# Block products on sums of blocks for six of the eleven chunks of each gated feed-forward (one Trainium2 core)

## What is computed

```
def swiglu(h, wg, wu, wd):
    return (jax.nn.silu(h @ wg) * (h @ wu)) @ wd

for l in range(DEPTH_2):                       # 2 layers
    h = rmsnorm(x, g[0])
    x = x + 0.5 * rmsnorm(swiglu(h, ffn_wg[l, 0], ffn_wu[l, 0], ffn_wd[l, 0]), g[1])
    ...                                        # mixer
    h = rmsnorm(x, g[4])
    x = x + 0.5 * rmsnorm(swiglu(h, ffn_wg[l, 1], ffn_wu[l, 1], ffn_wd[l, 1]), g[5])
```

## Time and profile before

| | |
|---|---|
| runs | 1431.85, 1432.91, 1433.77 us |
| profiled execution | span 1431.2 us, first to last instruction |
| TensorE busy | 1392.6 us, 97% |
| TensorE weight loads busy | 1157.8 us, 81% |
| VectorE busy | 926.0 us, 65% |
| ScalarE busy | 758.1 us, 53% |
| GpSimd busy | 79.3 us, 6% |
| mean granted TensorE clock | 0.993 |

### The profile page before, as it was taken

How to read it: one execution, slowest core, us unless ns; L and a number is a source line. 1 busy time by engine, 2 the same in 40 slices (tenths; PEclk the granted TensorE clock), 3 DMA queues, 4 the chain that set the end, 5 groups by cost and what they waited for, 6 DMA issues and landing times.

```text
span 1431.2 us, 19205 instructions
## 1 busy us (share of the span) xinstructions
PE 1392.6 (97%) x7039; PEld 1157.8 (81%) x7039; DVE 926.0 (65%) x1401; ACT 758.1 (53%) x1249; POOL 79.3 (6%) x133
## 2 busy tenths in 40 slices
PE   4999999999999999999899999999999999999998
PEld 4878877999988888887778888888888877788886
DVE  5677787799777554479986555476545556675453
ACT  4456746755456444366576444465444467574442
POOL 3011100000000000021300000000000100000000
PEclk9999999999999999999999999999999999999999
DMA  9887656477645765544355765547555373565550
GB/s 352 279 293 263 195 173 195 146 268 245 227 146 176 231 196 181 177 133 148 118 173 178 226 199 181 176 134 257 183 185 197 121 210 118 191 230 182 188 165 30
DMA packets 177596, 274.36 MB, mean 192 GB/s; under 512 B 6465, under 2 KB 120897, under 8 KB 177505
## 3 DMA queue, kind: packets, MB, share of 16 engines
q1 hardware_dynamic: 170800, 250.87, 53.2%
q0 software_dynamic: 5552, 20.20, 4.6%
q10 hardware_dynamic: 1153, 2.07, 0.4%
HBM read 272.05 MB, written 1.06 MB: 191 GB/s over the span
## 4 chain that ended last, share of the span: by engine, by line
PE 78%; DVE 4%; issue 1%; ACT 1%; POOL 0%; DVEq 0%; POOLq 0%; ACTq 0%
PE psum L2552 22%; PE psum L2554 22%; PE psum L2553 22%; PE psum L2595 2%; PE psum L2594 2%; PE psum L2592 2%; PE psum L2797 1%; DVE w_lo L2147 1%; PE psum L2649 1%; PE psum L2721 1%; PE psum L2750 0%; DVE attn L2324 0%; PE psum L2664 0%; DVE work L2301 0%; PE psum L2703 0%
## 5 line engine op out<-in xcount | busy, mean ns | idle before, releaser
L2147 DVE TENSOR_TENSOR w_lo<-raw,w_hi 128x1024 fp32r<-128x1024 f32 (+1 forms) x312 | 371.9, 1235 | 115.4 <-ACT w_hi L1936 114.5
L2552 PE MATMUL psum<-w_hi,hT_hi 128*128 128x512 f32 x888 | 357.3, 402 | 6.4 <-DVE hT_lo L2247 3.7
L1936 ACT ACTIVATE w_hi<-raw 128x1024 fp32r<-128x1024 f32 (+1 forms) x312 | 310.8, 1050 | 98.6 <-PE psum L2554 62.2
L2554 PE MATMUL psum<-w_hi,hT_lo 128*128 128x512 f32 x888 | 347.8, 392 | 0.0
L2553 PE MATMUL psum<-w_lo,hT_hi 128*128 128x512 f32 x888 | 347.3, 391 | 0.0
L2552 PEld LDWEIGHTS psum<-w_hi,hT_hi 128*128 128x128 f32 x888 | 167.8, 189 | 45.5 <-issue 10.2
L2554 PEld LDWEIGHTS psum<-w_hi,hT_lo 128*128 128x128 f32 x888 | 167.5, 189 | 36.5
L2553 PEld LDWEIGHTS psum<-w_lo,hT_hi 128*128 128x128 f32 x888 | 168.1, 189 | 32.8 <-issue 0.5
L2147 DVE TENSOR_TENSOR lo_qk<-raw,hi_qk 128x1024 fp32r<-128x1024 f32 (+1 forms) x72 | 84.1, 1209 | 32.5 <-ACT hi_qk L1936 31.8
L2552 PE MATMUL psum<-w_hi,hc_hi 128*128 128x512 f32 x256 | 100.3, 392 | 0.6 <-DVE hc_lo L2472 0.6
L2554 PE MATMUL psum<-w_hi,hc_lo 128*128 128x512 f32 x256 | 99.8, 390 | 0.0
(11 more groups left out here) (236 smaller groups left out, 2335.5 us busy)
## 6 DMA issues: line engine op xcount, KB each, us to landing
raw<-in_ffn_wg_dram SPq DMA_DIRECT2D x88, 512.0 KB, 4.0
raw<-in_ffn_wu_dram SPq DMA_DIRECT2D x88, 512.0 KB, 5.0
raw<-in_ffn_wd_dram SPq DMA_DIRECT2D x44, 1024.0 KB, 5.0
raw<-in_w_up_dram SPq DMA_DIRECT2D x44, 512.0 KB, 4.9
raw<-in_w_in_dram SPq DMA_DIRECT2D x19, 1024.0 KB, 7.5
ada_raw<-in_w_ada_dram POOLq DMA_DIRECT2D x24, 512.0 KB, 5.1
raw<-in_even_w_in_dram SPq DMA_DIRECT2D x12, 1024.0 KB, 5.1
raw<-in_odd_w_in_dram SPq DMA_DIRECT2D x12, 1024.0 KB, 5.5
```

Source lines behind the costliest of these rows:

```text
L1936: nc.scalar.activation(hi_of(s)[:, cs], raw_of(s)[:, cs], ACT.Copy).then_inc(ready, 1)
L2147: nc.vector.tensor_tensor(lo_of(u)[:, cs], raw_of(u)[:, cs], hi_of(u)[:, cs].bitcast(F32), ALU.subtract)\
L2552: nc.tensor.matmul(o, a_hi, b_hi, start=start, stop=False)
L2554: return nc.tensor.matmul(o, a_lo, b_hi, start=False, stop=stop)
```

## The change

Chunks 2 and 3, 5 and 6, 8 and 9 of each gated feed-forward form three *groups* (`GROUPS`). The up product of a group is seen as a product of 2 x 2 blocks: the tokens are 2 token tiles x 2 halves of the inputs, the weights 2 halves of the inputs x (512 gate columns, 512 up columns). It is computed with seven block products in place of eight (the scheme of Strassen and Winograd), on sums and differences of blocks:

- once per feed-forward, VectorE adds `hT_hi` and `hT_lo` back to float32 and forms four mixed token blocks in `gate_rows` (step `mixed_rows`: two instructions of 128x1024, four of 128x512, each waiting for the one before); ScalarE writes their high part, one instruction of 128x2048, and VectorE their low part, one of 128x2048 (step `mixed_split`);
- per group, four of the seven weight blocks are made by VectorE as differences (`form`, two instructions of 128x1024 each), three of them in the buffer `scr` and one in place in `raw`; all seven are then split as units are. The seven products (`gprod`) take 4 x 3 matmuls of 128x128x512 each, 84 against 96 before. In the order of use they are here called products 1 to 7: gate block; up minus gate; other up block minus that; that minus the second; (down product of the chunk before); the third's raw block; the other gate block; and the last difference;
- VectorE and ScalarE put the products together: `gkeep` (ScalarE, two copies 128x512), `gsum` (VectorE, three sums 128x512), `gup` (one), `ggate` (ScalarE two silus, VectorE one sum and two multiplications, 128x512);
- the hidden values of a group are transposed later (`gturn`), between the halves of the up product of the chunk that follows, and the down product of the group's first chunk comes behind that chunk's up product; the third group's second half goes into `tail`;
- a `raw` buffer is held until the last block that needs it has been split (`release`).

The diff, cut to what is spoken of:

```diff
+GROUPS = (2, 5, 8)
+MORE = 3 * len(GROUPS)
+UNITS = 228 + 4 * MORE
...
@@ FfnHead.go_on
+            pl.add("mixed_rows", g=self.G[KT - 1, 1])
             self.down(0)
+            pl.add("mixed_split")
             self.hidden_turn(1)
-            for c in range(2, NFC - 1):
+            c = 2
+            while c < NFC - 1:
+                if c in GROUPS:
+                    self.group(c)
+                    c += 2
+                    continue
+                after_group = c - 2 in GROUPS
                 self.up(c, 0)
+                if after_group:
+                    self.group_turn(c - 2, 0)
                 self.up(c, 1)
+                if after_group:
+                    self.group_turn(c - 2, 1)
                 self.out(c)
+                if after_group:
+                    self.down(c - 2)
                 self.down(c - 1)
                 self.hidden_turn(c)
+                c += 1
+
+        def group(self, c):
...
+            u1 = pl.unit(4, BANK, [(0, BANK, block(gate, 0))])
+            u5 = pl.sum_unit(block(up, 0), "sums", "own", u1)
+            u7 = pl.sum_unit(block(up, 4), u5, "own", u5)
+            u6 = pl.sum_unit(None, "sums", u7, "sums")
+            pl.release[u1], pl.release[u5] = u5, u7
...
+            product_of(u1, p1, True, tile=(0, 0), mixed=None)
+            product_of(u5, p5, True, tile=None, mixed=3)
+            pl.add("gkeep", use=p1, slot=0)
+            product_of(u7, p7, True, tile=None, mixed=2)
+            pl.add("gkeep", use=p5, slot=1)
+            product_of(u6, p6, True, tile=None, mixed=0)
+            pl.add("gsum", kept=(p1, p5), uses=(p6, p7), n=n)
+            self.down(c - 1)
+            u3 = pl.unit(4, BANK, [])
+            pl.raw_from[u3], pl.release[u7] = u7, u3
...
@@ FfnHead.tail
+            if c - 2 in GROUPS:
...
+                product_step("up", p, ks=(0, 1), inc=None)
+                for t in range(TT):
+                    self.group_turn(c - 2, t)
+                product_step("up", p, ks=(2, 3))
+                self.down_part(c - 2)
@@ SyncE
-                        sp.wait_ge(hi_ready, number + 1)
-                        sp.wait_ge(lo_ready, number + 1)
+                        until = plan.release.get(number, number)
+                        sp.wait_ge(hi_ready, until + 1)
+                        sp.wait_ge(lo_ready, until + 1)
@@ VectorE, split_lo(s)
+                form(s + 1)
                 for half in range(2):
                     split_lo_half(s, half)
@@ TensorE
+                elif kind == "gprod":
+                    use, u = a["use"], a["unit"]
+                    wait_free(pe, use)
+                    if a["mixed"] is not None:
+                        pe.wait_ge(tokens_split, n_mixed[0])
...
```

More of the change, by code:

```diff
@@ L143, in __init__ @@
         self.vars, self.x_parts = 0, 0
+        self.formed, self.raw_from, self.release = {}, {}, {}
+        self.n_group, self.last_sum = 0, None
         self.stat_cols = 0
@@ L152, in unit, with sum_unit @@
         return len(self.units) - 1
+    def sum_unit(self, load, dst, a, b):
+        u = self.unit(4, BANK, [(0, BANK, load)] if load is not None else [])
+        a, b = (u if v == "own" else v for v in (a, b))
+        self.formed[u] = dict(no=len(self.formed), dst=dst, a=a, b=b, last=self.last_sum if dst == "sums" else None)
+        if dst == "sums":
+            self.last_sum = u
+        return u
     def use(self, bank, unit=None, read_by=None, by_unit=False):
@@ L245, in load_order @@
         for kind, a in self.steps:
-            if kind == "split_hi" and a["unit"] < len(self.units):
+            if kind == "split_hi" and a["unit"] < len(self.units) and self.units[a["unit"]][2]:
                 order.append(("w", a["unit"]))
@@ L751, in build_plan, with __init__ @@
     class FfnHead(Head):
-        def __init__(self, turn_args, banks0, banks1, up_units, conv, w_down, during=(), before_end=()):
+        def __init__(self, turn_args, banks0, banks1, up_units, conv, w_down, during=(), before_end=(), gate_up=None):
             Head.__init__(self, turn_args, banks0, banks1)
+            self.gate_up = gate_up
+            self.singles = [c for c in range(NFC) if conv or not any(g <= c < g + 2 for g in GROUPS)]
             self.during, self.before_end = list(during), before_end
@@ L906, in tail @@
             c = NFC - 1
-            self.up(c, 0)
+            if c - 2 in GROUPS:
+                self.units[c] = self.up_units(c, (0,))
+                self.down_unit(c - 2)
+                self.units[c] += self.up_units(c, (4,))
+                self.open(c)
+                p = self.parts[c][0]
+                pl.split_ahead(p["unit"])
+                product_step("up", p, ks=(0, 1), inc=None)
[3 more added lines that the diff above has]
+                self.down_part(c - 2)
+            else:
+                self.up(c, 0)
             second = self.parts[c][1]
@@ L1698, in hidden_of, with group_hidden_of @@
             return buf[:, c % 2, :].rearrange("p (f s) -> p f s", f=2)[:, :, ts[0] * P:(ts[-1] + 1) * P]
+        def group_hidden_of(buf, c, t):
+            order = buf[:, :, :] if c % 2 == 0 else buf[:, ::-1, :]
+            return order.rearrange("p b (f s) -> p b f s", f=2)[:, :, :, t * P:(t + 1) * P]
         def col(st, part, i):
@@ L1717, in raw_of, with source_of @@
             return raw[:, raw_slot["w", u], 0:width(u)]
+        def source_of(u):
+            if u in plan.formed:
+                dst = plan.formed[u]["dst"]
+                return blended if dst == "sums" else raw_of(dst)
+            return raw_of(plan.raw_from.get(u, u))
         def half_of(u, half):
@@ L1935, in split_hi @@
                     cs = half_of(s, half)
-                    nc.scalar.activation(hi_of(s)[:, cs], raw_of(s)[:, cs], ACT.Copy).then_inc(ready, 1)
+                    if made is not None:
+                        act.wait_ge(sum_ready, 2 * made["no"] + half + 1)
+                    nc.scalar.activation(hi_of(s)[:, cs], source_of(s)[:, cs], ACT.Copy).then_inc(ready, 1)
+            n_mixed = [0]
             def turned_mod(a):
@@ L2137, in split_lo, with form @@
                     return
+                form(s + 1)
                 for half in range(2):
                     split_lo_half(s, half)
+            formed = set()
+            def form(u):
+                if u not in plan.formed or u in formed:
+                    return
+                formed.add(u)
+                made = plan.formed[u]
+                for v in (made["a"], made["b"]):
+                    if v != "sums" and v not in plan.formed or v == u:
+                        dve.wait_ge(weight_loaded[raw_slot["w", v]], landed["w", v])
+                if made["dst"] == "sums":
+                    if made["last"] is not None:
+                        dve.wait_ge(hi_ready, made["last"] + 1)
+                        dve.wait_ge(lo_ready, made["last"] + 1)
+                if made["no"]:
+                    dve.wait_ge(sum_ready, 2 * made["no"])
+                plus, minus = raw_of(made["a"]), blended if made["b"] == "sums" else raw_of(made["b"])
+                for half in range(2):
+                    cs = half_of(u, half)
+                    nc.vector.tensor_tensor(source_of(u)[:, cs], plus[:, cs], minus[:, cs], ALU.subtract).then_inc(sum_ready, 1)
             def split_lo_half(u, half):
```

175 lines of the change are left out of this document (165 added, 10 removed).

## The result

The changed kernel takes 1490.69 us, the median of four runs (1485.92 to 1497.78), against 1432.79 us for the kernel before: a ratio of 1.0407, 95% interval [1.0377, 1.0437]. The forecast was 1480, the range 1456 to 1510. The profiled execution is one of the longer ones, with a span of 1496.0 us, 64.8 above the 1431.2 of before.

A forecast was written before the change was run, and what follows sets the result against it. TensorE was taken to bound the kernel: span 1431.2 - 32.6 (matmuls) + 62 (wait at feed-forward starts) + 17.6 (waits behind groups) = 1478.2, the median 1.7 above: 1480 us, range 1456 to 1510.

The forecast's parts named there:

- Taken from TensorE: Each group has 84 matmuls instead of 96, at 0.227 us a step: 32.6 us saved in all, 8.2 per feed-forward.
- Prices on VectorE: Step times for VectorE's added work: 2.27 us per pair forming a block, `hc_lo` 0.60; 43.6 us per group and following chunk.
- Place 1: Start of each feed-forward: TensorE waits 15.5 us before product 2 for the mixed tokens' low part, 62 us in all.
- Place 2: Behind groups: TensorE waits for hidden values 2.3, 1.3 and 0.8 us, 4.4 per feed-forward, 18 in all.
- The low clock: Behind place 1's wait: eight half-rate matmuls, 1.6 us, counted inside place 2; 6 us more in all if nothing hid it.
- A: Rival: TensorE stays the bound, VectorE finishing its chain by 463; 1400 us, or 1409 with half of place 2; chance 0.06.
- B: Rival: VectorE binds in every period, 3 to 4 us more per group, gaps at every block product; 1522 us, chance 0.14.
- C: Rival: place 1's wait as computed, nothing at place 2; 1462 us, chance 0.2.

The follow-up runs named there:

- turns-first order: Changed kernel with VectorE writing the second hc_lo before the next weights' low part behind the first and second groups: 1476.67 us, 1.0300 of the kernel before.
- the first run: Changed kernel with the mixed tokens' low part moved directly behind their sums: 1496.41 us, 1.0436 of the kernel before.

## Why the prediction was right, and what it mis-sized

**Taken from TensorE: right.** 6895 instructions, 144 fewer. The step is 0.227 where the clock is full. With two groups and the mixed tokens in three pieces, where hardly a wait is left, the gain per removed matmul is 4.3 / 24 = 0.18 us.

**Prices on VectorE: right.** A pair that forms a block steps by 2.27 (453.13 to 455.40), and the chain from `hc_lo` to the end of `mixed_lo` came out as 453.13 to 478.17, for 453.7 to 478.6.

**Place 1: right in size, incomplete in reason.** 62.1 us in four waits, for 62. I called it "arithmetic of one engine", and the runs bear that out: a reordering changed only the name of the wait, an idle stretch used took off 2.1, less work took off 4 (forms) or turned it into a wait of 5.2 for `hc_lo` (no tokens). What I had not seen is that ScalarE's order is a second limit 3 us underneath.

**Place 2: near in sum, for partly other reasons.** Forecast 17.6 us; measured 13.6 at the groups and 3.0 in the tail, 16.6. Behind the first group I had 2.3 each time and found 0.93, 3.30, 1.71 and 0.86; behind the second I had 1.3 and found 0.91, 1.92, 0.89 and 3.08. The four above one us hang on loads: there VectorE waits 2.50, 0.91, 0.95 and 1.92 us for a `raw` buffer (6.3 in all), and in the other four it waits for none. For the largest, VectorE's row first, then TensorE's:

```profile
840.37 2.36 DVE L2319 TENSOR_TENSOR scr<-raw 128x1024 f32<-128x1024 f32 x2 [2.50 <-DMA raw<-in_ffn_wu_dram]
```

```profile
850.80 0.50 PE L2799 MATMUL psum<-hi_at,hc_hi 128*128 128x512 f32 x1 [3.30 <-DVE hc_lo L2418]
...
852.74 0.63 PE L2800 MATMUL psum<-lo_at,hc_hi 128*128 128x512 f32 x1
```

Late loads or not, all of it could be avoided: with one low part out of the way between the two `hc_lo`, 0.2 us were left. That low part stood in my chain ("form 34.2, split 36.4, second 37.1"), and I did not ask whether it had to.

**The low clock: the mis-sized term.** The step was "it falls into a stretch in which VectorE is behind (place 2), so I count it once, inside that", hence no term of its own. Measured in the profiled run: 70 slow matmuls in seven groups of 8 to 13, 0.427 us each, 13.8 us more than at full clock. Four groups (9.1 us) stand behind the place-1 waits, where I had 8 matmuls each and 6 us "if nothing hid it"; three (4.7 us) behind the larger waits of place 2, which I had not thought of. The first part is not simply hidden. VectorE does not run through from place 1 to place 2 whatever TensorE does: in each feed-forward ScalarE waits 3.43 us for TensorE, and VectorE 1.3 to 1.7 us for ScalarE, which is at most 0.4 us where the clock was kept up. How much of the 9.1 us reaches the end no run settles. What I summed as 4.4 us per feed-forward for place 2 and clock came out as 3.4 + 0.75 waiting and 3.5 slow, 7.6. That is 13 of the 19 us by which the feed-forwards grew beyond the 11.7 each forecast.

As means of four: 163.7 - 8.2 for matmuls + 15.5 + 3.4 + 0.75 + 3.5 = 178.7, against 180.1. Of the 1.4 left, about 1 stands at the edges of the waits: the last matmul before one runs its 0.39 us where its step would be 0.227, and the step behind one is 0.57 us at place 1 (478.35 to 478.92) and 0.33 at place 2. The median stands 5 us below the profiled run, so that the forecast was off by 11 us only.

**The rivals.** A (1400) would have needed VectorE to be through by 463; it was at 478. B (1522) needed waits at every block product: none stands there. C (nothing at place 2, 1462) is what the turns-first order makes, and it takes 1477: C, like my sum, has no term for place 1's slow matmuls (6.1 us in all there) and the edges of the waits, and the tail's 2.9 stay.

**Open.** The changed kernel's four runs spread over 12 us, those with turns first over 2.5. Late loads that hit a VectorE without slack would do that (in the run with added matmuls they hit other groups than in the changed kernel's trace), but no run tells it apart. Nor is it shown why the first run and the one with added matmuls stand 6 us above the changed kernel; their intervals overlap with its own. Three groups with the mixed tokens made in pieces were not tried.

## What to carry over

When work moves from the busiest engine to another, don't ask for that engine's average; take each pair of points at which the busy engine waits for it, add up what it has to do between them in its order, and compare. If it has no gap in between, only less work or work moved outside helps, and if a gap follows, putting the awaited piece first is free. Ask too where that engine waits for the busy one in turn, since a delay there comes back. Work that nobody waits for still delays what is queued behind it on an in-order engine, so cut it into pieces that fit the slack of a period: the same 7.5 us cost 7.0 us a feed-forward more in one piece (166.4 against 159.4, 4.8 of it waiting) than in three.

## What the runs showed of the hardware

- GpSimd and VectorE on large float32 sums: GpSimd 3.2 us for 128x1024, and VectorE's 1.14 us step grew to 2.2 to 3.0 beside it. From 1.29 us for 128x512 on GpSimd I had expected 2.5 and no effect on VectorE. GpSimd did take 2.4 where it began first; then VectorE's instruction took 3.3.
- After waits of 15.1 to 15.7 us, 9 to 13 matmuls stepped by 0.427 us, at the lower level of the clock.
- The price of a short wait is not fixed. After waits of 3.30 and 3.08 us the first six matmuls ran at nearly the full step and the next eight slowly (from 852.31 on in the first case); after 1.92 us five did, and the next eight were slow; after 1.71, 0.93 and less there were none. In the run with groups at 5 and 8, waits of 2.78 and 2.79 us had slow matmuls at once, and one of 2.80 us had none.
